# Row scales of a norm applied after the pointwise layer, and the last feed-forward unit summed by column halves

## The reference, cut to what matters

```python
x = x + jnp.square(jax.nn.relu(rmsnorm(x, l0_norm_ffn) @ l0_ffn_up)) @ l0_ffn_down
h = rmsnorm(x, l1_norm_mix)            # x * rsqrt(mean(x*x, -1) + 1e-6) * g
u = jax.nn.glu(h @ pw1 + pw1_b, -1)    # pw1: 1024 x 2048; a * sigmoid(b)
u = lax.conv_general_dilated(u, dw[:, None, :], (1,), [(30, 0)], ...) + dw_b   # 31 taps, one filter per channel
# then a layer norm over channels, silu, and u @ pw2 + pw2_b
```

## Time and profile before

| | us |
|---|---|
| median of 3 runs | 1093.39 (1091.84 to 1093.6) |
| the profiled execution's own time | 1094.86 |
| its span, first to last instruction | 1093.1 |
| PE busy | 1000.1 (91%) |
| PEld busy | 889.5 (81%) |
| DVE busy | 580.9 (53%) |
| ACT busy | 452.9 (41%) |
| mean granted TensorE clock | 0.943 of 2.4 GHz |

### The profile page before, as it was taken

The page is one execution under the profiler, slowest core; times in us unless marked ns, Lnnn a source line. Parts: engine busy times, 40 slices in busy tenths (PEclk is TensorE's granted clock), DMA queues, the critical chain, the costliest instruction groups (busy, mean ns, idle before and its releaser), DMA issues.

```text
span 1093.1 us, 16977 instructions
## 1 busy us (share of the span) xinstructions
PE 1000.1 (91%) x7278; PEld 889.5 (81%) x7278; DVE 580.9 (53%) x711; ACT 452.9 (41%) x620; POOL 42.9 (4%) x86
## 2 busy tenths in 40 slices
PE   4999999998899995998899999999889589999996
PEld 4898788897698784997778999998877369998995
DVE  4456656456545478344437555556533286555554
ACT  5445554444444563221035444444432255444442
POOL 6000000000110002100000000000100000000000
PEclk9999999999989897897599999999999889999998
DMA  9663344455556231000014565656556145565530
GB/s 307 196 196 118 125 145 135 136 185 183 182 174 184 86 116 39 2 1 1 1 40 150 197 193 174 200 170 199 167 160 176 27 135 165 182 195 191 193 116 39
DMA packets 108714, 152.52 MB, mean 140 GB/s; under 512 B 4050, under 2 KB 86368, under 8 KB 108640
## 3 DMA queue, kind: packets, MB, share of 16 engines
q1 hardware_dynamic: 101120, 141.45, 40.0%
q10 hardware_dynamic: 5296, 4.79, 1.9%
q0 software_dynamic: 2224, 5.20, 1.5%
HBM read 145.58 MB, written 1.06 MB: 134 GB/s over the span
## 4 chain that ended last, share of the span: by engine, by line
PE 85%; DVE 5%; issue 5%; ACT 3%; DMA 1%; POOL 0%; POOLq 0%; SPq 0%; ACTq 0%; DVEq 0%
PE banks L1607 22%; PE banks L1608 22%; PE banks L1609 22%; PE banks L1932 4%; PE banks L2069 3%; PE banks L1982 1%; PE banks L1961 1%; ACT wh L602 1%; PE banks L1736 1%; PE banks L1725 1%; PE banks L1719 1%; PE banks L1718 1%; DMA raw<-in_w_in 1%; PE banks L1967 1%; PE banks L1867 1%
## 5 line engine op out<-in xcount | busy, mean ns | idle before, releaser
L999 DVE TENSOR_TENSOR wl<-raw,wh 128x2048 fp32r<-128x2048 f32 x132 | 302.2, 2291 | 213.7 <-ACT wh L602 212.8
L1607 PE MATMUL banks<-xh,wh 128*128 128x256 f32 x1216 | 345.5, 284 | 2.0 <-DVE xl L1047 1.8
L1608 PE MATMUL banks<-xl,wh 128*128 128x256 f32 x1216 | 342.5, 282 | 0.0
L1609 PE MATMUL banks<-xh,wl 128*128 128x256 f32 x1216 | 342.2, 281 | 0.0
L602 ACT ACTIVATE wh<-raw 128x2048 fp32r<-128x2048 f32 x132 | 252.1, 1911 | 126.0 <-PE banks L1609 121.9
L1607 PEld LDWEIGHTS banks<-xh,wh 128*128 128x128 f32 x1216 | 230.6, 190 | 8.5 <-issue 7.2
L1608 PEld LDWEIGHTS banks<-xl,wh 128*128 128x128 f32 x1216 | 230.3, 189 | 1.3
L1609 PEld LDWEIGHTS banks<-xh,wl 128*128 128x128 f32 x1216 | 230.6, 190 | 0.0
L1607 PE MATMUL banks<-wh,yh 128*128 128x512 f32 x288 | 113.2, 393 | 1.8 <-DVE yl L1466 1.8
L1608 PE MATMUL banks<-wl,yh 128*128 128x512 f32 x288 | 112.2, 390 | 0.0
L1609 PE MATMUL banks<-wh,yl 128*128 128x512 f32 x288 | 112.2, 390 | 0.0
(11 more groups left out here) (289 smaller groups left out, 1115.8 us busy)
## 6 DMA issues: line engine op xcount, KB each, us to landing
raw<-in_l_ffn_up SPq DMA_DIRECT2D x32, 1024.0 KB, 5.5
raw<-in_l_ffn_down SPq DMA_DIRECT2D x32, 1024.0 KB, 5.0
raw<-in_w_in SPq DMA_DIRECT2D x29, 1024.0 KB, 5.3
raw<-in_l_w_in SPq DMA_DIRECT2D x13, 1024.0 KB, 5.2
raw<-in_l_pw SPq DMA_DIRECT2D x12, 1024.0 KB, 5.4
arena<-arena ACTq DMA_DIRECT2D x64, 71.0 KB, 3.0
raw<-in_w_out SPq DMA_DIRECT2D x4, 1024.0 KB, 5.1
raw<-in_l_w_out SPq DMA_DIRECT2D x4, 1024.0 KB, 5.0
```

The source lines that it names most:

```text
L999: nc.vector.tensor_tensor(wl[:, u % WBUFS, :], raw[:, u % RAWS, :], wh[:, u % WBUFS, :].bitcast(F32), ALU.subtract).then_inc(E("lo_split"), 1)
L1607: mm(out, hh, mh, start=start, stop=False)
L1608: mm(out, hh, ml, start=False, stop=False)
L1609: return mm(out, hl, mh, start=False, stop=stop)
```

## The change

Four things are done. (1) The last down unit of `f0` runs in the order (0,0), (1,0), (0,1), (1,1), and TensorE transposes the finished column half (channels 0 to 511) of the unscaled rows before it starts (1,1); the other half is transposed behind it. The split into high and low parts follows by halves, and `pa0` takes its channels by halves. (2) The scale of each row is no longer multiplied into the rows. VectorE multiplies it into two identity blocks (`scale_diag`), TensorE multiplies these with a matrix of ones behind `pa0` (bank 7, use `rb`), and ScalarE copies the result, a tile that holds the 256 row scales in every partition, to `row_scale`. (3) VectorE takes `pa{i}` and `pb{i}` out of their banks and multiplies them by that tile (`scaled`); ScalarE's Identity and Tanh then work in place in SBUF. (4) The squares of the rows come behind ScalarE's split of the transposed rows. The copy of `rb` stands ahead of ScalarE's first weight split of the layer.

```diff
@@ plan @@
     norm("n4")
+    s.use("rb", 7)
@@ build @@
+        row_scale, scale_diag = arena[:, 4352:4608], arena[:, 4608:4864]
@@ ScalarE @@
-                if residual and not residual.startswith("dn"):
+                if residual and residual != "dnf1":
                     order = [(0, 0), (1, 0), (0, 1), (1, 1)]
...
             ffn("f0", 0, "wp")
+            split_norm("n4")
             squares("dnf0")
-            split_norm("n4")
+            copy_out(row_scale, "rb", T)
...
-                    wait_full(act, f"{tag}{i}")
+                    wait_empty(act, f"{tag}{i}")
                     for j in range(2):
-                        ins = nc.scalar.activation(dst[:, 0, j * T:(j + 1) * T], bank(f"{tag}{i}")[:, j * T:(j + 1) * T],
-                                                   fn, scale=scale, bias=bias(2 * i + j))
...
+                        h = dst[:, 0, j * T:(j + 1) * T]
+                        nc.scalar.activation(h, h, fn, scale=scale, bias=bias(2 * i + j)).then_inc(E("glu_parts"), 1)
@@ VectorE @@
+                if tag == "f1":
+                    add(0, 0), add(0, 1), add(1, 0), add(1, 1)
+                else:
+                    add(0, 0), add(1, 0), add(0, 1)
+                    split_norm("n4", (0, 1))
+                    add(1, 1)
+                    split_norm("n4", (2, 3))
             ffn("f0", 0)
-
-            scale_rows()
-            split_norm("n4")
+            dve.wait_ge(E("squares_summed"), summed[0] + 4)
+            for t in range(NT):
+                mean_squares(t).then_inc(E("mean_square"), 1)
+            summed[0] += 4
+            for t in range(NT):
+                nc.vector.tensor_scalar(scale_diag[:, t * P:(t + 1) * P], ident, rstd_of(t), None, ALU.mult)\
+                    .then_inc(E("scale_diag"), 1)
             dve.wait_ge(E("pad_zeroed"), 16)
+            rows2 = row_scale.rearrange("p (o t) -> p o t", o=1).broadcast_to([P, 2, T])
+
+            def scaled(tag, i, dst):
+                wait_full(dve, f"{tag}{i}")
+                nc.vector.tensor_tensor(chunks(dst[:, 0, 0:512]), chunks(bank(f"{tag}{i}")), rows2, ALU.mult)\
+                    .then_inc(empty(f"{tag}{i}"), 1)
...
             def glu(i):
-                wait_empty(dve, f"pa{i}")
-                wait_empty(dve, f"pb{i}")
-
+                dve.wait_ge(E("glu_parts"), 4 * i + 4)
...
             for i in range(4):
                 next_unit()
+                if i == 0:
+                    wait_empty(dve, "rb")
+                else:
+                    dve.wait_ge(E("glu"), i)
+                scaled("pa", i, ytmp)
                 next_unit()
                 build_taps(i)
+                scaled("pb", i, thb)
                 glu(i)
@@ TensorE @@
-                        wait_empty(pe, f"{residual}{c}_{s}")
+                        wait_empty(pe, f"{residual}_{2 * s + c}" if residual == "dnf0" else f"{residual}{c}_{s}")
...
+                    order = [(0, 0), (0, 1), (1, 0), (1, 1)]
+                    if tag == "f0" and j == FF_STEPS - 1:
+                        order = [(0, 0), (1, 0), (0, 1), (1, 1)]
+                    for s, c in order:
+                            if order[1][0] and (s, c) == (1, 1):
+                                row_transposes("n4", "dnf0", 0)
...
             ffn("f0", 0)
-            norm_transposes("n4")
+            row_transposes("n4", "dnf0", 1)
+
+            def broadcast_scale():
+                pe.wait_ge(E("scale_diag"), 2)
+                give(mm(take("rb")[:, 0:T], const("ones"), scale_diag, start=True, stop=True), "rb")
...
             for i in range(4):
-                t_unit(f"pa{i}", None if i else "n4")
+                t_unit(f"pa{i}", None if i else "n4", halves=not i)
+                if i == 0:
+                    broadcast_scale()
                 t_unit(f"pb{i}")
                 if i:
                     conv_taps(i - 1)
```

More of the change, by code:

```diff
@@ L1488, in ffn @@
                 sync()
[L1489 to L1495, removed]
@@ L1497, in _, with add @@
-            ffn("f0", 0)
-            scale_rows()
-            split_norm("n4")
-            dve.wait_ge(E("pad_zeroed"), 16)
+                def add(s, c):
+                    name = f"dn{tag}_{2 * s + c}"
+                    wait_full(dve, name)
+                    nc.vector.scalar_tensor_tensor(out=xn[:, s, 512 * c:512 * c + 512], in0=bank(name),
+                                                   scalar=RSQ[:, s:s + 1], in1=xn[:, s, 512 * c:512 * c + 512],
+                                                   op0=ALU.mult, op1=ALU.add).then_inc(empty(name), 1)
@@ L2042, in ffn @@
                     buf = 2 * (j % 3)
-                    for s in range(NT):
-                        for c in range(2):
+                    order = [(0, 0), (0, 1), (1, 0), (1, 1)]
[4 more added lines that the diff above has]
+                                row_transposes("n4", "dnf0", 0)
                             b = 4 + 2 * s + c
```

## The result

The changed kernel takes 1102.95 us (median of 4 runs, 1099.17 to 1104.9), the kernel before 1092.8 us (4 runs, 1091.84 to 1093.6): ratio on record 1.0075, 95% interval 1.0052 to 1.0097. The quotient of the two medians is 1.0093 and lies in that interval. So the change costs 10 us by the medians and 8 by the ratio (6 to 11 by its interval). The forecast was 1103.3.

What follows compares the result with a forecast made beforehand. The prediction took the ring of VectorE, ScalarE and its DMA copies as the bound: first lap 4.7 plus three laps 5.2 gives 9.9 us, on 1094.86 makes 1104.8, less 1.5 for the median 1103.3; range 1098.8 to 1106.5.

Steps and rivals of the forecast that it cites:

- What bounds the kernel: Every us by which the fourth batch of copies starts later is a us of the kernel; forecast 9.9 us later.
- the ring: VectorE, ScalarE and its 16 DMA copy issues, each waiting on the other; laps averaged 18.8 us before.
- The handover: From the last down unit to pa0: pa0 starts 2.9 us earlier, worth nothing unless the fourth batch moves.
- The first lap: From the copy of rb to the first batch of copies: starts at 789.9 instead of 785.16, 4.7 us later.
- C: Rival: quicker DMA issue and GpSimd powers, the low ends of the unseen costs; 1099 to 1101.3 us, 9%.
- B: Rival: copies wait behind the splits on ScalarE; 1106.0 us, by their full ends 1107.5; 13%.
- The laps: Each further lap grows 1.7 us by scaled pb, the tanh pair and longer SBUF operations; three laps 5.2 us.
- the unseen costs: DMA issue overlap 0 to 2.7 us, powers -0.8 to +0.5, issue time -2 to +1, failed early transposes +2.9.
- What I took at nothing: ScalarE's DMA issues behind a split still in work: taken as 0 us, with ends 0 and 2.7.
- The slack on TensorE: Bank waits (pb1 1.3 us, then some 8 for the first copies) and slower first taps fit before the fourth batch.
- The last term: After the fourth batch of copies starts, nothing changes to the end of the kernel.
- The price of SBUF sources: Identity or Tanh takes 495 ns from SBUF, 473 from PSUM: 22 ns by the row, against 43 estimated.

Runs made afterwards that it cites:

- e1: Changed kernel with pb taken out and scaled before the taps are built, not after: median 1098.63 us, ratio to before 1.0034.
- e4: Changed kernel without the multiplication by the row scales, ScalarE reading the banks directly: median 1094.23 us, ratio to before 0.9985.
- e5: Changed kernel with the copy of the broadcast scales behind ScalarE's first weight split of the layer: median 1099.29 us, ratio to before 1.0043.
- e3: Kernel before with the taps built ahead of VectorE's second weight split of each pass: median 1093.47 us, ratio to before 0.9973.
- e2: Changed kernel with the taps built ahead of VectorE's second weight split of each pass: median 1093.94 us, ratio to before 0.9987.
- e6: Changed kernel with each group's 16 copies issued from two queues, 8 by ScalarE and 8 by SyncE: median 1091.37 us, ratio to before 0.9959.
- e7: Changed kernel with the edits of e2, e5 and e6 together: median 1083.86 us, ratio to before 0.9893.
- e8: Kernel before with the early taps of e3 and copies issued from two queues: median 1084.26 us, ratio to before 0.9901.

## Why the prediction was right

Counted from the first addition, forecast and measured stand like this.

| step | forecast | measured |
|---|---|---|
| pa0 | 6.0 | 5.8 |
| copy of rb | 12.6 | 12.7 |
| first batch of copies | 27.4 | 27.5 |
| lap, mean | 20.5 | 20.2 |
| fourth batch of copies | 89.1 | 88.1 |
| last taps | 101.5 | 100.6 |

**What bounds the kernel: right.** The fourth batch started 9.0 us later and the kernel became 9.6 us slower from the first addition on. e1, e4 and e5, which take away 4.2, 9.4 and 3.1 us of the ring and leave the handover's order as it is, show that it was these us and not the transposes between the sums.

That the forecast came within 0.4 us of the median (1103.3 and 1102.95) is in part luck: the laps came out 1.0 us shorter than forecast and the last taps 0.4 us longer, the four runs spread over 5.7 us, and the ratio's interval is 5 us wide. What the traces bear out is the table above, step by step.

**The handover: right**, 3.1 us for 2.9, and worth nothing, as said: pa0 three us earlier left the copies 4.8 us later.

**The first lap: right**, 4.8 us for 4.7. That ScalarE's split of pa1 stands behind the copy of the scales was named in the working; e5 puts 3.1 us on it. The table load (777.43 to 778.71) fell in ScalarE's wait for the scaled product, which lasted to 782.58, at no cost. One reading in the working is wrong and harmless: the "eight entries" of the row at 863.36 are not four matmuls and four weight loads. The timeline there has eight MATMULs and, apart, eight LDWEIGHTS for four fp32 matmuls, two of each for one. The price of one, a quarter of 1.94 us, stands; the broadcast's pair at 768.77 took 0.70 us from start to end, and the copy of `rb` started 0.1 us later than forecast. Of the rivals' times, 1099 as the low end of C and 1107.5 in B don't follow from the terms given; the low ends shown, -0.8 and -2, make 1100.5.

**The laps: the mechanism right, the size a little high.** Each of the three gained 1.66 us between taps and glu (forecast 1.65) and the Identity pair is 0.91 and no longer 0.84 (0.07, as forecast). Three laps took 60.6 us and before 56.5, which makes 4.2 and not 5.2, because issuing three batches took 31.9 us (10.46 + 10.99 + 10.42) and not the 32.9 of before, the 11.15 of rows 3 and these two (timeline of ScalarE, before):

```profile
804.16 10.96 ACTq L915 DMA_DIRECT2D arena<-arena  x16
...
822.97 10.80 ACTq L915 DMA_DIRECT2D arena<-arena  x16
```

The prediction had this in the unseen costs, with up to -2. In e1 the same three took 31.7, in e3 33.8; I can't say what sets it.

**What I took at nothing.** ScalarE's DMA issues behind a split: right at 0. The row at 824.87 begins 0.14 us into the split that starts at 824.73. So rival B, copies that wait for the end of splits, falls. The Trainium skill, TensorE: Matmul & The Clock Gate, section Architectural detail, calls ScalarE's queue a strict FIFO. The rows agree with it on the order of the starts (824.73, then 824.87), but not if it is taken, as in B, to mean that a DMA issue waits until the ACTIVATE ahead of it has ended. The slack on TensorE held as well: the first taps took 9.28 us and no longer 8.39, and the third group waited 2.24 us and took 8.80 and no longer 7.04, all inside the wait for the fourth batch.

**The last term**, "from there nothing changes", was right to 0.6 us: the last taps took 9.75 for 9.32 us, and the rest is within 0.2.

**The price of SBUF sources.** In place, Identity and Tanh took 502 and 500 ns:

```profile
L942 ACT ACTIVATE ytmp<-ytmp,vt 128x256 f32<-128x256 f32 x8 | 3.6, 502 | 31.2 <-issue 28.2 <-DVE ytmp L1518 3.0
L942 ACT ACTIVATE thb<-thb,small 128x256 f32<-128x256 f32 x8 | 3.6, 500 | 19.4 <-DVE thb L1518 19.4
```

The same view of before has Identity from the bank:

```profile
L937 ACT ACTIVATE ytmp<-banks,vt 128x256 f32<-128x256 f32 x8 | 3.4, 471 | 40.1 <-issue 36.9 <-PE banks L1609 3.2
```

From the bank they took 471 (this row) and 473 ns (Tanh), so SBUF costs 31 and 27 ns more. That lies between the row's 22 and the 43 that I had worked out as an estimate from the Trainium skill, VectorE: DVE Perf Modes, section The TRN2 errata, and nearer to the row.

## What to carry to other kernels

Where two engines and a DMA queue hand work around in a ring, an operation put between two of its steps costs its full time in every lap, however idle its engine is on average. Here VectorE was busy 53% of the kernel before, and still the scaled product's 0.69 us and the 0.97 us behind it counted in every lap. With the product one place further up (e1), the tanh ran beside the tap blocks and the 0.97 us were gone; with the tap blocks in VectorE's idle time (e2), their 2.2 us left the ring. Before moving work off a "busy" path, list for each step what is serial behind it, and put what depends on nobody (the tap blocks, a weight split) ahead of what waits. And when a bound is taken away, count the next one by its whole chain: in e6, behind the halved DMA issues, it was the chain that starts with pa3 and the time until the copies were there, not TensorE alone.

## What the runs showed of the hardware

The granted clock of an unchanged stretch differs between executions by enough to matter. From 300 to 400 us the two programs do the same work; the profile by stretch has (us, PE, PEld, DVE, ACT, POOL busy with counts, PEclk, DMA share, GB/s), before and then after:

```profile
300.00:400.00 100.00, 97.18 (x638) 86.60 (x639) 55.59 (x88) 53.13 (x86) 3.48 (x5) 0.90 0.44 139
```

```profile
300.00:400.00 100.00, 97.18 (x668) 87.16 (x667) 58.56 (x93) 57.34 (x94) 2.40 (x4) 0.95 0.44 141
```

The clock is 0.90 in one and 0.95 in the other, and most of the 5.7 us by which the execution of after was ahead at the first addition came about by the end of this stretch: VectorE's line 1266 starts for the first time at 347.0 us in the one and at 344.8 in the other, and for the last time at 407.4 and 402.7. That the clock alone made this lead is not shown. Behind nearly equal gaps (2.90 and 2.04 us) the last taps of e7 ran at a mean clock of 0.81 and those of e8 at 1.00, 8.80 against 7.11 us:

```profile
843.08:851.88 8.80, 8.80 (x129) 5.87 (x129) 0.00 (x0) 0.00 (x0) 0.00 (x0) 0.81 0.01 2
```

```profile
846.73:853.84 7.11, 7.11 (x129) 4.95 (x129) 0.00 (x0) 0.00 (x0) 0.00 (x0) 1.00 0.01 2
```

So differences of one or two us between kernels are to be read between fixed points of the same chain, and not from the spans of two executions.
